# Strassen's algorithm in layer 0's queries and keys and its last two convolved blocks

## The chip, the cores and the metric

The kernel runs on one core of a Trainium2 chip. The metric is the device time of one execution in microseconds (us), as a median over runs; the profile shows one further execution of the same program.

## The reference

Two layers of a hybrid backbone over 256 context and 512 latent tokens of 1024 features, all in float32. Each layer normalises and modulates its input, multiplies it by one wide input projection, and feeds three groups of heads: a state space mixer (SSD) behind a three-tap convolution, differential attention, and latent attention (MLA). An output projection and an expert-choice mixture of 16 experts follow. What matters here is the input projection and what reads it first:

```python
ssd_l, diff_l, mla_l = jnp.split(h_lat @ w_in, cuts, axis=-1)
q, k, v = jnp.split(p, 3, axis=-1)                # differential attention, 256 columns each
k1 = jnp.concatenate([k1c, rope_2d(k1l, rows, cols)], axis=1)
xbc = jax.nn.silu(centred_dwconv(xbc, conv_w, conv_b))   # SSD: 512 columns of x, 128 of B, 128 of C
```

## The kernel before

`hT` holds the modulated rows of all 768 tokens, features on the partitions: 8 k-tiles of 128 features. Products that give features on the partitions take 128 columns of the projection as the stationary operand and tokens as the moving one (`feature_major`, L2468: two spans of 512 and 256 tokens, eight matmuls each); the values are made token by token (`token_major`, L2480).

Each engine has its own program, written out by hand in the order of the work, and they meet at semaphores. A PSUM slot is one of four tiles of 1024 floats; the jobs that use them are numbered by `job_plan` (L179) and job j has slot j modulo 4. `J.empty(j)` waits until the slot's last user has freed it, `J.filled(j)` and `J.freed(j)` for the job's own two steps. In layer 0 the queries and keys are jobs 11 to 14 ("qk"), their rotations 15 to 18 ("rot"), the values 19 and 20 ("v"). The convolved blocks are jobs x+0, 1, 3, 4, 5, 7 and the modulation rows (2, 1) and (2, 2) jobs x+2 and x+6.

Weights come through a ring of four buffers of 2 MB. SP issues the loads in the order of L822, and before it refills a buffer it waits in `block_used` (L788) for the last product with what lies there:

```python
for b in [*range(10), 11, 10, 12, 13, 15, 14, *range(16, PRE_BLOCKS)]:
```

Load 4 holds the weights of the queries and keys, 5 those of the values, 10 those of the first four convolved blocks, 15 those of the last two. Loads 12, 13, 14 and 16 hold modulation weights for `block_rows(l, 2, 0)` to `(l, 2, 3)` (L2497). Load b goes to buffer b modulo 4, so 14 goes where 10 was.

Layer 0 up to the first scores (TensorE L2638 to L2709): four blocks by `feature_major`, each followed by the rotation of the block before it (`quarter_turned`, L2640, one product with a constant matrix); values of four tiles, the last rotation, values of two tiles; then the first scores. ScalarE takes the queries and keys out of PSUM (L1167 to L1173): latents into `QK`, context heads into `QH` and `KH`. VectorE (L1682 to L1697) multiplies each block by cosines, its rotation by sines, and adds.

The convolved blocks of both layers come later (TensorE L2850 to L2894, VectorE L1862 to L1998, ScalarE L1301 to L1329). The first four are already made by Strassen's algorithm in Winograd's form: with tokens halved into 2 x 384, features into 2 x 512 and channels into pairs of blocks, seven products of half size take the place of eight. VectorE makes four sums of rows (`TH`, 1536 columns) and four of weights (`SW`, 1024), and joins the products out of PSUM by short sums of 384 columns. ScalarE copies the first product of a pair out (`E1`). These steps are counted by `half_products`, `half_sums` and `half_out`. Then, block by block in the order 2, 0, 3, 1, 4, 5, ScalarE scales with the middle tap, VectorE adds the other two taps (L1987) and ScalarE applies Silu. Blocks 4 and 5 are plain `feature_major` products, with `block_rows(l, 2, 2)` between them. Behind them on TensorE: sums over time, `block_rows(l, 2, 3)`, turned sums, the first gate with the columns of the modulation (`block_column`, which waits for VectorE's `rows_added(l, 2, 3)`), and the turning of all convolved blocks (L2931).

Of the kernel before, what the change touches and what calls it, by code (L numbers as in the profile page):

```python
# [24 lines left out]
P = 128  # L25
# [454 lines left out]
def build(nc, T, out):  # L480
    JOB = JOBS
    with ExitStack() as ctx:
# [117 lines left out]

        HT = TOK // 2
# [8 lines left out]
        CONV_ORDER = (2, 0, 3, 1, 4, 5)  # L610
# [431 lines left out]
        def _(act):  # L1042
# [109 lines left out]
            for l in range(DEPTH):  # L1152
# [14 lines left out]
                for m in range(4):  # L1167
                    j, scale = jb("qk") + m, DQ ** -0.5 if m < 2 else 1.0
                    act.wait_ge(*J.filled(j))
                    ins = act.activation(QK[:, m, CTX:TOK], J.tile(j)[:, CTX:TOK], ACT.Copy, scale=scale)  # L1170
                    if l == 0:
                        ins = context_heads_out(QH if m < 2 else KH, m % 2, J.tile(j)[:, 0:CTX], scale)
                    ins.then_inc(*J.free(j))  # L1173
# [127 lines left out]
                products0, sums0 = 10 * l, 22 * l  # L1301
# [11 lines left out]
                for i, m in enumerate(CONV_ORDER):  # L1313
                    j = conv_job(l, m)
                    if m in (2, 3):
                        act.wait_ge(S["half_sums"], sums0 + (15, 20)[m - 2])
                    elif m < 2:
                        act.wait_ge(*J.freed(conv_job(l, 2 * m + 1)))
                    else:
                        act.wait_ge(*J.filled(j))  # L1320
                    on = slice(conv_start(l, m), TOK)
                    src = CM[m] if m < 4 else J.tile(j)
                    act.activation(XB[:, m, on], src[:, on], ACT.Identity, bias=pc[:, R_CB + m:R_CB + m + 1],
                                   scale=pc[:, R_CW + CONV_T + m:R_CW + CONV_T + m + 1]).then_inc(S["conv_mid"], 1)
                    if m < 4:
                        act.wait_ge(S["half_sums"], sums0 + (16, 19, 21, 22)[i])
                    else:
                        act.wait_ge(*J.freed(j))
# [256 lines left out]
        def _(dve):  # L1585
# [56 lines left out]
            for l in range(DEPTH):  # L1642
# [33 lines left out]
                dve.tensor_reduce(lam[:, 128:130], view(lam[:, 0:64], a=2), AX_X, ALU.add).then_inc(S["lam_dots"], 1)  # L1676
                dve.wait_ge(*v.next(S["lam_exps"]))
# [4 lines left out]
                for m in range(4):  # L1682
                    dve.wait_ge(*J.freed(jb("qk") + m))
# [182 lines left out]
                sums0, out0, products0 = 22 * l, 2 * l, 10 * l  # L1866
# [1630 lines left out]
```

## Time and profile before

| | |
|---|---|
| three runs | 2092.53, 2095.02, 2096.34 us; median 2095.02 |
| profiled execution | 2094.3 us, span 2092.2 us, mean granted clock 0.988 |
| TensorE | matmuls in flight 1942.3 us (93%) |
| VectorE, ScalarE, GpSimd | 721.6 us (34%), 519.1 (25%), 186.9 (9%) |
| DMA | 530.64 MB, mean 254 GB/s |

Times in rows are us from the start of the span. A float32 matmul stands in the trace as two instructions. The length of a row of matmuls goes to the modelled end of its last one, which overlaps the next row; so the distance of two starts tells what work costs. "idle before" with an engine and a line is the time that the engine stood still, and what ended it. The clock is the granted clock of TensorE: 1.00 is 2.4 GHz, 0.5 is 1.2 GHz. A value between is a stretch with both.

### The profile page before, as it was taken

The page shows a single profiled execution, that of the slowest core. Times are in us where ns is not written, and L with a number is a line of the kernel's source. Part 1 is how long each engine was busy: PE and PEld are TensorE (multiplying, and loading weights), DVE is VectorE, ACT ScalarE, POOL GpSimd, SP SyncE. Part 2 cuts the span into 40 slices and gives each one's busy share as a digit, 9 for nine tenths or more (in the row PEclk, how much of TensorE's full clock was granted, in tenths as well). Part 3 has the DMA queues.
Part 4 walks back from the last instruction along what each step waited for, and adds up shares of the span by engine and source line. Part 5 has one row for each costly group of instructions (what it writes and reads, how often), then busy time and mean ns, then how long its engine had stood idle before and what let it go on. Part 6 is the DMA issues. An engine that isn't in the chain of part 4 may idle for free. (4 is left out here: it accounts for less than half of the span.)

```text
span 2092.2 us, 25952 instructions
## 1 busy us (share of the span) xinstructions
PE 1942.3 (93%) x10858; PEld 934.4 (45%) x10858; DVE 721.6 (34%) x1335; ACT 519.1 (25%) x1020; POOL 186.9 (9%) x216
## 2 busy tenths in 40 slices
PE   5998999989989999999999999999898998888886
PEld 2656565544433333333334866655445333232222
DVE  2258565372431110111113476563624111111113
ACT  4146552452300000000003255524321100000012
POOL 1300000120011111212012000001100000000000
PEclk9999999999999999999999999999999999999999
DMA  9520304222289999999999223024419999999996
GB/s 351 147 81 1 141 1 152 90 105 96 82 343 401 393 399 395 394 401 393 402 395 301 111 82 141 1 90 153 165 61 357 395 408 408 408 409 409 409 409 261
DMA packets 164805, 530.64 MB, mean 254 GB/s; under 512 B 11016, under 2 KB 19538, under 8 KB 164690
## 3 DMA queue, kind: packets, MB, share of 16 engines
q1 hardware_dynamic: 149344, 489.49, 60.0%
q0 software_dynamic: 15120, 39.43, 6.1%
q8 instruction: 87, 1.43, 0.3%
q14 instruction: 28, 0.23, 0.0%
q10 hardware_dynamic: 226, 0.07, 0.0%
HBM read 507.98 MB, written 20.97 MB: 253 GB/s over the span
## 5 line engine op out<-in xcount | busy, mean ns | idle before, releaser
L3267 PE MATMUL ps<-ring,arena 128*64 128x512 f32 x1040 | 233.2, 597 | 13.6 <-DMA ring<-in_w_up 8.8
L3267 PE MATMUL ps<-arena 128*64 128x512 f32 x720 | 165.0, 604 | 3.6 <-DMA arena<-in_w_gate 3.2
L3267 PEld LDWEIGHTS ps<-ring,arena 128*64 128x64 f32 x1040 | 72.1, 137 | 161.6 <-issue 141.3
L3093 PE MATMUL ps<-ring,arena 128*128 128x512 f32 x320 | 141.6, 597 | 1.0 <-ACT arena L1442 0.6
L2366 DVE TENSOR_TENSOR arena<-arena,ps 128x512 f32<-128x512 f32 x32 | 22.0, 688 | 280.1 <-ACT arena L1487 280.1
L3316 PE MATMUL ps<-ring,arena 128*64 128x512 f32 x496 | 112.4, 596 | 5.8 <-DMA ring<-in_w_down 5.8
L2476 PE MATMUL ps<-arena,ring 128*128 128x256 f32 (+1 forms) x384 | 110.4, 447 | 2.5 <-DMA ring<-in_w_in 2.5
L1487 ACT ACTIVATE arena<-ps 128x512 f32<-128x512 f32 x32 | 19.1, 597 | 373.4 <-PE ps L3267 373.4
L3316 PE MATMUL ps<-arena 128*64 128x512 f32 x432 | 97.9, 595 | 5.2 <-DMA arena<-in_w_down 4.5
L1066 ACT ACTIVATE arena<-ps 128x768 f32<-128x768 f32 (+6 forms) x111 | 79.9, 724 | 88.0 <-PE ps L2494 45.3
L3267 PEld LDWEIGHTS ps<-arena 128*64 128x64 f32 x720 | 50.4, 139 | 107.0 <-issue 100.3
L2476 PEld LDWEIGHTS ps<-arena,ring 128*128 128x128 f32 x384 | 73.2, 191 | 41.1 <-issue 31.5
L3093 PEld LDWEIGHTS ps<-ring,arena 128*128 128x128 f32 x320 | 59.7, 191 | 70.3 <-issue 69.5
L3216 PE MATMUL ps<-ring,arena 128*32 128x512 f32 x624 | 86.0, 594 | 0.4 <-DVE arena L2160 0.4
L2494 PE MATMUL ps<-const,arena 128*128 128x128 f32 x524 | 77.0, 283 | 7.9 <-DVE arena L1832 5.5
L1196 ACT ACTIVATE arena<-ps,nmax 128x768 f32<-128x768 f32 (+1 forms) x80 | 64.5, 811 | 60.6 <-DVE nmax L1715 56.1
L1715 DVE TENSOR_REDUCE nmax<-ps 128x1 f32<-128x768 f32 (+1 forms) x80 | 64.3, 846 | 39.8 <-PE ps L2682 38.9
L2494 PEld LDWEIGHTS ps<-const,arena 128*128 128x128 f32 x524 | 58.4, 143 | 42.5 <-issue 23.9
L2312 DVE TENSOR_TENSOR arena<-arena,ps 64x512 f32<-64x512 f32 x16 | 11.1, 692 | 188.7 <-ACT arena L1483 188.7
L2156 DVE TENSOR_TENSOR arena<-ps,coef 128x512 f32<-128x512 f32 (+1 forms) x48 | 28.8, 600 | 128.0 <-PE ps L3192 127.4
L3316 PEld LDWEIGHTS ps<-ring,arena 128*64 128x64 f32 x496 | 34.2, 137 | 77.3 <-issue 72.0
L914 POOL DMA_INDIRECT arena<-normed_rows,small x32 | 33.3, 1039 | 394.2 <-PE ps L3192 356.9
(417 smaller groups left out, 2821.8 us busy)
## 6 DMA issues: line engine op xcount, KB each, us to landing
ring<-in_w_up SPq DMA_DIRECT2D x33, 2048.0 KB, 14.7
ring<-in_w_gate SPq DMA_DIRECT2D x32, 2048.0 KB, 21.1
ring<-in_w_down SPq DMA_DIRECT2D x30, 2048.0 KB, 23.0
ring<-in_ada_w SPq DMA_DIRECT2D x24, 2048.0 KB, 9.9
arena<-in_w_down SPq DMA_DIRECT2D x19, 2048.0 KB, 23.2
arena<-in_w_gate SPq DMA_DIRECT2D x18, 2048.0 KB, 22.5
arena<-in_w_up SPq DMA_DIRECT2D x12, 2048.0 KB, 13.6
ring<-in_w_in SPq DMA_DIRECT2D x6, 2048.0 KB, 14.0
```

Source lines behind the costliest of these rows:

```text
L914: pool.indirect_dma_start(got_l[e % 2], None, halves_in, at_rows(e, 0)).then_inc(got_lat[e % 2], 16)
L1066: act.activation(dst, src, func, scale=scale).then_inc(*J.free(j))
L1196: act.activation(by_halves(PD[u % 2][m], t, nk // 2), by_halves(J.tile(j), t, 512), ACT.Exp, bias=nmax[:, c:c + 1], accum_out=esum[:, c:c ...
L1715: dve.tensor_reduce(nmax[:, c:c + 1], by_halves(J.tile(j), t, 512), AX_X if t < CT else AX_XY, ALU.max, negate=True).then_inc(S["negmax"], 1)
L2156: TT(x4, src.rearrange("p (c h n) -> p c h n", h=parts, n=n), cF[:, :, s].rearrange("p (h c) -> p c h", h=parts).unsqueeze(3) .to_broadcas ...
L2366: TT(hid_l, hid_l, px[0][:, 512:1024], ALU.mult).then_inc(S["hid_lat"], 1)
L2476: ins = mm(o[0:n, c0:c1], w[:, k, col:col + n], hT[:, k, c0:c1], start=k == 0, stop=k == KD - 1)
L2494: ins = pe.transpose(o[:, k * P:(k + 1) * P], src(k), ident)
L3093: ins = mm(o[:, hf * 512:(hf + 1) * 512], mix, wo[hf][:, k, :], start=k == 0, stop=k == KD - 1)
L3216: ins = mm(px[1][32 * i:32 * i + 32, 0:512], xc[e % 2][:, at:at + CAP_C], w[c][:, hf * 512:hf * 512 + 512], start=b + c == 0, stop=b * c == 3)
L3267: ins = mm(px[0][hf * 64:hf * 64 + 64, col:col + 512], xl[e % 2][:, at:at + CAP_L], w[c][:, hf * 512:hf * 512 + 512], start=b + c == 0, st ...
L3316: ins = mm(px[1][hf * 64:hf * 64 + 64, 512:1024], hT_l[0][:, at:at + CAP_L], w[c][:, hf * 512:hf * 512 + 512], start=b + c == 0, stop=b * ...
```

## The change

Layer 0's queries and keys are made by the same algorithm as the first convolved blocks, 14 products of four k-tiles and 384 tokens in place of four whole blocks; the pairs are blocks (0, 2) and (1, 3). VectorE makes eight sums from rows and weights and fourteen out of PSUM; ScalarE copies each pair's first product, later scales the latents of the query blocks in place, and copies the context heads from `QK`. Rotation 2 is put between the twelfth and the thirteenth product, rotation 0 behind the last product, 3 and 1 between the tiles of the values. The first scores wait for two roped blocks where they waited for three.

Layer 0's last two convolved blocks are made by seven such products. `block_rows(0, 2, 2)` stands behind the first of them. VectorE makes four sums of weights (512 columns each) within its turn for block 3; ScalarE copies the first product before its turn for block 1; the order of the blocks becomes 2, 0, 3, 1, 5, 4. In both layers `rows_added(l, 2, 1)` moves from behind block 1's taps to before `early_half(0)`; in layer 0 `rows_added(0, 2, 2)` moves before block 5's sums. SP's program is unchanged.

The diff, cut to its core, with eight columns of indentation taken off:

```diff
+def half_counts(l, conv):
+    return (25, 51, 9) if l else (10, 18, 6) if conv else (0, 0, 0)
+def qk_ready(m):
+    return S["half_out"], (4, 6, 3, 5)[m]
+QKH = (TOK - query_tiles(0)[0] * P) // 2
...
-CONV_ORDER = (2, 0, 3, 1, 4, 5)
+CM += [CM[0], CM[2]]
+CONV_ORDER = ((2, 0, 3, 1, 5, 4), (2, 0, 3, 1, 4, 5))
...
+            products0, sums0, _ = half_counts(l, 0)
+            for p in range(2):
+                act.wait_ge(S["half_products"], products0 + p + 1)
+                act.activation(EQ[p], J.tile(jb("qk") + 2 * p)[:, 0:QKH], ACT.Copy).then_inc(S["half_out"], 1)
+            for m in (2, 0, 3, 1):
+                scale = DQ ** -0.5 if m < 2 else 1.0
+                if m < 2:
+                    act.wait_ge(*J.freed(jb("qk") + 2 * m + 1))
+                    act.activation(QK[:, m, CTX:TOK], QK[:, m, CTX:TOK], ACT.Copy, scale=scale)
+                else:
+                    act.wait_ge(S["half_sums"], sums0 + (15 if m == 2 else 18))
+                context_heads_out(QH if m < 2 else KH, m % 2, QK[:, m, 0:CTX], scale).then_inc(S["half_out"], 1)
...
+            if l == 0 and m == 1:
+                act.wait_ge(S["half_products"], products0 + 11)
+                act.activation(E1[0], J.tile(conv_job(l, 4))[:, 0:HT], ACT.Copy).then_inc(S["half_out"], 1)
...
+        if l == 0:
+            qk_sum(TQ[0], qk_rows(0, 1), qk_rows(0, 0), ALU.subtract)
+            qk_sums_done(1)
+            qk_sum(TQ[1], qk_rows(4, 1), TQ[0], ALU.subtract)
+            dve.wait_ge(ring_full[n4 % RING], ring_turns(n4) * 16)
+            qk_sum(SQ[0], qk_weights(1, 0), qk_weights(1, 4))
+            qk_sums_done(3)
+            qk_sum(SQ[1], SQ[0], qk_weights(0, 0), ALU.subtract)
+            qk_sum(SQ[2], qk_weights(0, 0), qk_weights(1, 0), ALU.subtract)
+            qk_sum(TQ[2], qk_rows(4, 1), qk_rows(0, 1), ALU.subtract)
+            qk_sums_done(4)
+            qk_sum(SQ[3], qk_weights(0, 4), SQ[1], ALU.subtract)
+            qk_sum(TQ[3], qk_rows(4, 0), TQ[1], ALU.subtract)
+            for p in range(2):
+                dve.wait_ge(S["half_out"], out0 + p + 1)
+                dve.wait_ge(S["half_products"], products0 + 3 + p)
+                qk_sum(qk_out(p, 0), EQ[p], qk_tile(p, 0, 0))
+            for p in range(2):
+                dve.wait_ge(S["half_products"], products0 + 5 + p)
+                qk_sum(EQ[p], EQ[p], qk_tile(p, 0, 1))
+            for p in range(2):
+                qk_sums_done(11 + p)
+                dve.wait_ge(*J.filled(jb("qk") + 2 * p))
+                TT(UQ[p], EQ[p], qk_tile(p, 0, 1), ALU.add).then_inc(*J.free(jb("qk") + 2 * p))
...
+        def qk_late(p):
+            dve.wait_ge(*J.freed(jb("qk") + 2 * p))
+            dve.wait_ge(S["half_products"], products0 + 7 + 2 * p)
+            qk_sum(qk_out(2 + p, 1), UQ[p], qk_tile(p, 1, 0))
+            qk_sum(EQ[p], EQ[p], qk_tile(p, 1, 0))
+        def qk_early(p):
+            dve.wait_ge(S["half_products"], products0 + 8 + 2 * p)
+            qk_sum(qk_out(2 + p, 0), UQ[p], qk_tile(p, 1, 1))
+        def qk_last(p):
+            qk_sums_done((14, 17)[p])
+            dve.wait_ge(*J.filled(jb("qk") + 2 * p + 1))
+            TT(qk_out(p, 1), EQ[p], qk_tile(p, 1, 0), ALU.add).then_inc(*J.free(jb("qk") + 2 * p + 1))
+        if l == 0:
+            qk_late(0)
+            qk_early(0)
+            qk_last(0)
+            qk_late(1)
+        for i, m in enumerate(range(4) if l else (2, 0, 3, 1)):
+            if l == 0 and i == 1:
+                qk_early(1)
+                qk_last(1)
+            dve.wait_ge(*(J.freed(jb("qk") + m) if l else qk_ready(m)))
...
+        rows_added(l, 2, 1)
         early_half(0)
         last_half(0)
-        for m in CONV_ORDER:
+        def bc_weight_sums():
+            n15 = block_base(l) + 15
+            dve.wait_ge(ring_full[n15 % RING], ring_turns(n15) * 16)
+            wb15, s_ = ringv(n15), [last_pair_of_channels(x) for x in range(4)]
+            dve.wait_ge(*J.filled(conv_job(l, 2)))
+            half_sum(s_[0], wb15[:, 0:4, P:2 * P], wb15[:, 4:8, P:2 * P], ALU.add)
+            sums_done(21)
+            half_sum(s_[1], s_[0], wb15[:, 0:4, 0:P], ALU.subtract)
+            sums_done(22)
+            half_sum(s_[2], wb15[:, 0:4, 0:P], wb15[:, 0:4, P:2 * P], ALU.subtract)
+            half_sum(s_[3], wb15[:, 4:8, 0:P], s_[1], ALU.subtract)
+        def bc_halves():
+            j0, j1 = conv_job(l, 4), conv_job(l, 5)
+            dve.wait_ge(S["half_out"], out0 + 3)
+            rows_added(l, 2, 2)
+            dve.wait_ge(S["half_products"], products0 + 12)
+            half_sum(CM[4][:, 0:HT], E1[0], J.tile(j0)[:, 0:HT], ALU.add)
+            dve.wait_ge(S["half_products"], products0 + 13)
+            half_sum(E1[0], E1[0], J.tile(j0)[:, 512:512 + HT], ALU.add)
+            sums_done(28)
+            dve.wait_ge(*J.filled(j0))
+            TT(U3[0], E1[0], J.tile(j0)[:, 512:512 + HT], ALU.add).then_inc(*J.free(j0))
+            dve.wait_ge(*J.freed(j0))
+            half_sum(CM[5][:, HT:TOK], U3[0], J.tile(j1)[:, 0:HT], ALU.add)
+            half_sum(E1[0], E1[0], J.tile(j1)[:, 0:HT], ALU.add)
+            dve.wait_ge(S["half_products"], products0 + 15)
+            half_sum(CM[5][:, 0:HT], U3[0], J.tile(j1)[:, 512:512 + HT], ALU.add)
+            sums_done(30)
+            dve.wait_ge(*J.filled(j1))
+            TT(CM[4][:, HT:TOK], E1[0], J.tile(j1)[:, 0:HT], ALU.add).then_inc(*J.free(j1))
...
+        for m in CONV_ORDER[l]:
             j = conv_job(l, m)
             if m == 0:
                 late_half(1)
             if m == 3:
                 early_half(1)
+                if l == 0:
+                    bc_weight_sums()
                 last_half(1)
+            if m == 5 and l == 0:
+                bc_halves()
...
-            if m in (1, 4):
-                rows_added(l, 2, m // 2 + (m == 1))
+            if l and m == 4:
+                rows_added(l, 2, 2)
...
+            def qk_product(p, i, hf, a, b, k0=None):
+                o = J.tile(jb("qk") + 2 * p + i)[:, 512 * hf:512 * hf + n]
+                for k in range(4):
+                    if k0 is not None:
+                        first_h(k0 + k)
+                    ins = mm(o, a[:, k, :], b[:, k, :], start=k == 0, stop=k == 3)
+                return ins
+            def of_qk_pair(x, p):
+                return SQ[x][:, :, P * p:P * p + P]
+            for p in range(2):
+                pe.wait_ge(*J.empty(jb("qk") + 2 * p))
+                qk_product(p, 0, 0, qk_weight(p, 0, 0), qk_rows(0, 0), 0 if p == 0 else None).then_inc(S["half_products"], 1)
+            for p in range(2):
+                pe.wait_ge(S["half_out"], out0 + p + 1)
+                qk_product(p, 0, 0, qk_weight(p, 0, 4), qk_rows(4, 0), 4 if p == 0 else None).then_inc(S["half_products"], 1)
+            pe.wait_ge(S["half_sums"], sums0 + 4)
+            for p in range(2):
+                qk_product(p, 0, 1, of_qk_pair(1, p), TQ[1]).then_inc(S["half_products"], 1)
+            for p in range(2):
+                pe.wait_ge(S["half_sums"], sums0 + 11 + p)
+                qk_product(p, 0, 1, of_qk_pair(2, p), TQ[2]).then_inc(*J.fill(jb("qk") + 2 * p))
+            for p in range(2):
+                pe.wait_ge(*J.empty(jb("qk") + 2 * p + 1))
+                qk_product(p, 1, 0, of_qk_pair(0, p), TQ[0]).then_inc(S["half_products"], 1)
+                if p:
+                    quarter_turned(l, 2)
+                qk_product(p, 1, 1, qk_weight(p, 1, 4), TQ[3]).then_inc(S["half_products"], 1)
+                pe.wait_ge(S["half_sums"], sums0 + (14, 17)[p])
+                qk_product(p, 1, 0, of_qk_pair(3, p), qk_rows(4, 1)).then_inc(*J.fill(jb("qk") + 2 * p + 1))
+            quarter_turned(l, 0)
...
-            token_major(jb("v"), w[:, :, 0:256], range(0, 4), 256, 256)
-            quarter_turned(3)
+            token_major(jb("v"), w[:, :, 0:256], range(0, 4), 256, 256, between={1: 3, 2: 1})
             token_major(jb("v") + 1, w[:, :, 0:256], range(4, 6), 256, 256)
             pe.wait_ge(*J.freed(jb("v") + 1))
-        pe.wait_ge(*w_.next(S["qk_roped"], 3))
+        pe.wait_ge(*w_.next(S["qk_roped"], 3 if l else 2))
...
+            pe.wait_ge(*J.empty(conv_job(l, 4)))
+            bc_product(0, 0, w[:, 0:4, 0:P], rows_half(0, 0)).then_inc(S["half_products"], 1)
+            block_rows(l, 2, 2)
+            pe.wait_ge(S["half_out"], out0 + 3)
+            bc_product(0, 0, w[:, 4:8, 0:P], rows_half(4, 0)).then_inc(S["half_products"], 1)
+            pe.wait_ge(S["half_sums"], sums0 + 24)
+            bc_product(0, 1, last_pair_of_channels(1), TH[1]).then_inc(S["half_products"], 1)
+            pe.wait_ge(*J.empty(conv_job(l, 5)))
+            bc_product(1, 0, last_pair_of_channels(0), TH[0]).then_inc(S["half_products"], 1)
+            pe.wait_ge(S["half_sums"], sums0 + 28)
+            bc_product(0, 1, last_pair_of_channels(2), TH[2]).then_inc(*J.fill(conv_job(l, 4)))
+            bc_product(1, 1, w[:, 4:8, P:2 * P], TH[3]).then_inc(S["half_products"], 1)
+            pe.wait_ge(S["half_sums"], sums0 + 30)
+            bc_product(1, 0, last_pair_of_channels(3), rows_half(4, 1)).then_inc(*J.fill(conv_job(l, 5)))
```

The counts of the semaphores in layer 1 and in the convolution are shifted by what the new steps add; nothing else of layer 1's products changes.

## Rows read from the trace of the kernel before

**Rows 1.** The page: span, and busy time of TensorE, VectorE, ScalarE and GpSimd.

```profile
span 2092.2 us, 25952 instructions
...
PE 1942.3 (93%) x10858; PEld 934.4 (45%) x10858; DVE 721.6 (34%) x1335; ACT 519.1 (25%) x1020; POOL 186.9 (9%) x216
```

**Rows 2.** Windows of the experts: length, busy PE, PEld, DVE, ACT, POOL, clock, DMA.

```profile
800.00:900.00 100.00, 100.00 (x718) 36.06 (x716) 13.29 (x24) 7.41 (x12) 16.00 (x12) 1.00 1.03 397
...
1800.00:2092.00 292.00, 241.75 (x987) 79.92 (x985) 58.51 (x89) 32.84 (x57) 4.85 (x6) 0.97 0.96 383
```

**Rows 3.** Timeline of TensorE, layer 0's queries, keys, values: start, length, what, count [idle].

```profile
41.54 22.60 PE L2476 MATMUL ps<-arena,ring 128*128 128x512 f32 x64 [2.45 <-DMA ring<-in_w_in]
...
63.98 1.02 PE L2645 MATMUL ps<-arena,const 128*128 128x512 f32 x2
64.84 10.48 PE L2476 MATMUL ps<-arena,ring 128*128 128x512 f32 x32
75.16 1.02 PE L2645 MATMUL ps<-arena,const 128*128 128x512 f32 x2
...
109.63 0.70 PE L2682 MATMUL ps<-arena,resid 32*128 32x256 f32 x4 [0.69 <-ACT arena L1066]
```

**Rows 4.** Timeline of TensorE, layer 0, from the convolution's products to the turned blocks.

```profile
341.33 2.74 PE L2865 MATMUL ps<-arena 128*128 128x384 f32 x8
343.91 10.48 PE L2476 MATMUL ps<-arena,ring 128*128 128x512 f32 x32
354.32 1.92 PE L2508 MATMUL ps<-ring,silu_c 128*32 128x512 f32 x16
...
366.60 0.32 PE L2900 MATMUL ps<-small,const 128*128 128x48 f32 x2
...
374.15 0.28 PE L2532 MATMUL ps<-const,mod_rows 128*128 128x8 f32 x2
...
381.44 0.29 PE L2936 MATMUL ps<-const,arena 128*128 128x2 f32 x2
```

**Rows 5.** Timeline of VectorE beside the convolution of layer 0.

```profile
306.09 3.55 DVE L1881 TENSOR_TENSOR arena<-arena 128x1536 f32<-128x1536 f32 x2
...
317.56 0.55 DVE L1881 TENSOR_TENSOR arena<-arena,ps 128x384 f32<-128x384 f32 x1
...
343.31 0.55 DVE L1881 TENSOR_TENSOR arena<-arena,ps 128x384 f32<-128x384 f32 x1
344.18 0.56 DVE L1933 TENSOR_TENSOR resid<-arena,ps 128x384 f32<-128x384 f32 x1 [0.33 <-PE ps L2865]
345.22 2.33 DVE L1987 SCALAR_TENSOR_TENSOR resid<-arena,par,resid 128x255 f32<-128x255 f32 x4 [0.48 <-ACT resid L1323]
349.37 2.33 DVE L1987 SCALAR_TENSOR_TENSOR resid<-resid,par 128x255 f32<-128x255 f32 x4 [1.83 <-ACT resid L1323]
351.61 0.68 DVE L1615 TENSOR_TENSOR mod_rows<-ps,mod_rows 128x512 f32<-128x512 f32 x1
```

**Rows 6.** SP's timeline, then the transfers issued from 343.9 to 344.3 with landing.

```profile
344.10 0.99 SPq L835 DMA_DIRECT2D ring<-in_ada_w  x2
...
ring<-in_ada_w SPq DMA_DIRECT2D x1, 2048.0 KB, 7.8
```

**Rows 7.** Timeline of VectorE beside layer 0's queries and keys.

```profile
44.44 0.22 DVE L1676 TENSOR_REDUCE lam<-lam 128x2 f32<-128x64 f32 x1
...
65.77 2.79 DVE L1695 TENSOR_TENSOR resid<-arena 64x512 f32<-64x512 f32 x4
...
88.12 2.78 DVE L1695 TENSOR_TENSOR arena<-arena 64x512 f32<-64x512 f32 x4
```

**Rows 8.** Windows: beside the queries and keys, and around TensorE's idle at 1501.

```profile
44.40:68.00 23.60, 23.60 (x70) 13.36 (x69) 4.12 (x10) 4.18 (x11) 23.25 (x40) 0.96 0.81 203
...
1500.90:1504.20 3.30, 0.07 (x1) 0.00 (x0) 0.77 (x3) 3.08 (x13) 0.00 (x0) 0.91 0.59 237
1504.20:1510.80 6.60, 5.59 (x35) 4.51 (x36) 2.23 (x4) 1.74 (x5) 2.73 (x5) 0.53 0.79 302
```

More of the change, by code:

```diff
@@ L609, in build, with last_pair_of_channels, plain @@
         assert h0 + 4 * HT + TOK <= h1 - 704
-        CONV_ORDER = (2, 0, 3, 1, 4, 5)
+        CM += [CM[0], CM[2]]
+        CONV_ORDER = ((2, 0, 3, 1, 5, 4), (2, 0, 3, 1, 4, 5))
+        def last_pair_of_channels(x):
+            return SW[1 + x // 2][:, :, P * (x % 2):P * (x % 2) + P]
+        def plain(l, m):
+            return l > 0 and m >= 4
         XC = 640 + SG
@@ L2478, in feature_major, with quarter_turned, token_major @@
                             ins.then_inc(*J.fill(j))
-            def token_major(j, w, tiles, n, stride, at=0):
+            def quarter_turned(l, m):
+                j = JOB[l, "rot"] + m
+                pe.wait_ge(*(J.freed(JOB[l, "qk"] + m) if l else qk_ready(m)))
+                pe.wait_ge(*J.empty(j))
+                mm(J.tile(j)[:, 0:SEQ], kc(K_ROT), QK[:, m, CTX:TOK], start=True, stop=True).then_inc(*J.fill(j))
+            def token_major(j, w, tiles, n, stride, at=0, between={}):
                 pe.wait_ge(*J.empty(j))
@@ L2484, in token_major @@
                 for i, t in enumerate(tiles):
+                    if i in between:
+                        quarter_turned(0, between[i])
                     for k in range(KD):
@@ L2638, in _, with qk_weight, qk_rows @@
                 w = arrived(wb + 4)
-                def quarter_turned(m):
-                    j = jb("rot") + m
-                    pe.wait_ge(*J.freed(jb("qk") + m))
-                    pe.wait_ge(*J.empty(j))
-                    mm(J.tile(j)[:, 0:SEQ], kc(K_ROT), QK[:, m, CTX:TOK], start=True, stop=True).then_inc(*J.fill(j))
-                for m in range(4):
-                    feature_major(jb("qk") + m, w, m * P, P, t0,
-                                  ready=(latents_ready if l else first_h) if m == 0 else None)
-                    if m:
-                        quarter_turned(m - 1)
+                if l:
+                    for m in range(4):
+                        feature_major(jb("qk") + m, w, m * P, P, t0,
+                                      ready=latents_ready if m == 0 else None)
+                        if m:
+                            quarter_turned(l, m - 1)
+                else:
+                    _, sums0, out0 = half_counts(l, 0)
+                    n, c0 = QKH, t0 * P
+                    def qk_weight(p, half, k0):
+                        return w[:, k0:k0 + 4, 256 * half + P * p:256 * half + P * p + P]
+                    def qk_rows(k0, half):
+                        return hT[:, k0:k0 + 4, c0 + half * n:c0 + half * n + n]
+                    def qk_product(p, i, hf, a, b, k0=None):
[28 more added lines that the diff above has]
+                    quarter_turned(l, 0)
@@ L2675, in map_scores @@
                     if u == 2 * nq:
-                        pe.wait_ge(*w_.next(S["qk_roped"]))
+                        pe.wait_ge(*w_.next(S["qk_roped"], 1 if l else 2))
                     for m in range(2):
```

78 lines of the change are left out of this document (52 added, 26 removed).

## The prediction, made before the change was run

> **What bounds the kernel now.** I read the page first: the span is 2092.2 us and TensorE has matmuls in flight for 93% of it [rows 1]. The table by windows then says what an early saving is worth: in the expert stage of layer 0 TensorE never idles, and the end of layer 1 runs at the rate of the weight transfers (a DMA share of 0.96 with TensorE at 242 of 292 us) [rows 2]. Those transfers refill buffers that TensorE lets go, so an earlier or later TensorE in layer 0's mixer moves everything behind it one for one. I take that as the price of every microsecond below; its other bound is that the transfers hide it, which would only draw the result towards zero. Only TensorE's timeline in the two changed stretches counts, then: queries and keys with the values behind them [rows 3], and the last two convolved blocks with what follows [rows 4].
>
> **First part: queries and keys.** A block of 768 columns and eight k-tiles took 75.16 - 64.84 = 10.32 us [rows 3]. The kernel already does its first four convolved blocks by Strassen, and one product there (four k-tiles, 384 columns) took 343.91 - 341.33 = 2.58 us [rows 4]. Four blocks, 41.28 us, become 14 products, 36.12 us: **-5.16 us**. The four rotations stay, at 0.9 each.
>
> Do the sums come in time? I carried the old starting point: the first two blocks took 22.4 us where two take 20.6, so 1.8 us go at the start at the lower clock, in both versions. Product n then ends at 43.34 + 2.58n: product 4 at 53.7, product 6 at 58.8. VectorE is free after the reduction at 44.44 [rows 7]. The same eight sums took 317.56 - 306.09 = 11.47 us in the convolution [rows 5], the fourth being done halfway. Here the fourth is done at 50.6 (needed at 53.7), the eighth at 56.1; the three short ones behind it (0.5 us each, row 343.31) put the one that product 7 needs at 57.6, against 58.8. So there is no wait, with 1.2 us to spare. Block 2 (keys) is whole behind product 10 (69.1), ScalarE copies its context heads by 71.5, and its rotation comes at 74.3: no wait. The second pair follows the same pattern 7.7 us later, with the same covers.
>
> A new wait stands at the values. The job of the values has the PSUM slot of rotation 0 (19 and 15 modulo 4), and VectorE frees it only after the last product's sum. Product 14 ends at 80.3 (with rotation 2's 0.9); the sum reads it 0.27 later (344.18 - 343.91), takes 0.5, then cosine and sine product, 0.68 each as the row at 351.61: 82.5. TensorE has done rotation 0 at 81.2: **+1.3 us**. Rotations 3 and 1, now between value tiles, find their halves copied and their slots free (81 to 84 against 86 and 90). The rope additions (2.8 us a block) end near 95, the values near 105, and the first scores wait for ScalarE's copy of the values as before, 109.63 being 3.85 us too late now. Net **-3.85 us**.
>
> **Second part: the last two convolved blocks.** I keep the old times here; all of it comes 3.85 us earlier. Two blocks, 20.64 us, become seven products, 18.06 us: -2.6 us. But the order on TensorE changes as well. block_rows(0, 2, 2), which multiplies modulation weights from the ring, stood behind a whole convolved block (354.32 [rows 4]); now it stands behind one product, at 343.91 + 2.58 = 346.49. Its weights are load 14, in ring slot 2, where load 10 (the weights of the first four blocks) was; SP may refill it only when the last product with load 10 is done. The queue shows that: it issued at 344.10, and the 2 MB landed 7.8 us later, at 351.9 [rows 6]. Before, this was hidden by 2.4 us; now TensorE waits **5.4 us**, and everything is queued behind it in order. The change doesn't touch SP's order.
>
> That wait covers the other one. The copy E1[0], which product 2 needs, stands in ScalarE's queue behind block 3's Silu, which waits for VectorE's taps, and those now stand behind four new weight sums. From row 343.31: 0.5, four sums of 128x512 at some 0.7 (row 351.61, the nearest), 0.5, taps 2.24 (351.61 - 349.37), Silu and copy 1.3: 350.6, before 351.9. It costs nothing here; without the transfer it would be 350.6 - 346.5 - 1.9 = 2.3 us.
>
> So TensorE: 351.9 + 1.9 (row 354.32) + 6 x 2.58 = 369.2, against 366.60: **+2.6 us**. In these products each sum is ready at least 0.6 us ahead.
>
> Behind it, the end E of the convolution starts a chain for the two last blocks: last sum at E + 0.27, 0.5; taps of block 5, 2.24; Silu and scaling to the next taps 1.9 (349.37 - 345.22 - 2.24 [rows 5]); taps of block 4, 2.24; row addition 0.68; handed over at E + 7.9. TensorE asks for the finished rows at 374.15 - 366.60 = 7.55: **+0.35 us**. The turned blocks are asked for at E + 14.8 (381.44) and ready at E + 9: free. POOL and the next SP loads start some us later and have more than that to spare. The earlier row addition frees the PSUM slot that block_rows(l, 2, 2) needs, 0.7 us of VectorE in a gap; in layer 1, where nothing else changes, nobody waited there, so nothing.
>
> **The clock.** TensorE idle for 3.3 us at 1500.9 came back to 6.6 us at 0.53, the 1.2 GHz level, and then worked at 2.4 again [rows 8]. A 5.4 us idle stretch will do the like. Bounds are 0 and half of 6.6, 3.3 us; the work here is dense at once, unlike at 1504, so I take **+1.7 us**. The Trainium skill, "TensorE: Matmul & The Clock Gate", What's actually happening, calls the throttled state the default that activity releases; by that rule the fall would come here too, and the trace agrees.
>
> **Sum:** -3.85 + 2.6 + 0.35 + 1.7 = +0.8 us on 2094.3, the profiled execution's time (2.1 over its span, which I keep); that run stood 0.7 below the median of 2095.0, so the forecast is **2095.8 us**: no difference that can be told. A measurement here tells some 0.2%, 4.2 us, from nothing; the three runs lie 3.8 apart.
>
> **Rivals.**
> 1. *The transfer doesn't hold TensorE* (lands by 348.8). Then the copy's wait of 2.3 decides, the clock stays: -3.85 - 2.6 + 2.3 + 0.35 = -3.8, 2091.2. Against it: it would have to land 4.7 us after its issue where it took 7.8, or be released earlier, and the only thing that releases it is the last product. 0.10, half of it over the bound.
> 2. *Everything is hidden*: -5.2 - 2.6, 2087.2. Needs a free slot at the values and no wait in the convolution; the rows speak against both. 0.06.
> 3. *Slower: VectorE's sums come too late.* Place: before product 7, margin 1.2 us. POOL issues small loads from 44.7 to 68, just beside the eight sums; were the sums half as long again (5.7 us), TensorE would wait 4.5 and the time be 2100.3; doubled, 2106. It decides from sums 10% longer, and is slower than the bound from 40%. Against: four additions beside POOL's issues took 2.79 us (65.77), without them 2.78 (88.12) [rows 7]. 0.10. The Trainium skill, "SBUF — State Buffer", Who interferes with whom, says that a VectorE instruction with two SBUF inputs and a GpSimd instruction that reads SBUF block each other whole; by that rule this is the case to fear, but the trace shows no such stretch for queue issues.
>
> **Numbers.** The forecast case has 0.74. Its own spread (clock 0 to 3.3, values' wait 0 to 2.5, runs +-1.5) is 2092.5 to 2099; with rival 1 and the nearest of rival 3 the range is **2091.0 to 2099.5**. Faster by over 0.2%: 0.12; within: 0.76; slower: 0.12.
>
> **What would show it.** Right: TensorE idle some 5 us before line block_rows in the convolution, put down to the ring's transfer, then a stretch of clock near 0.5; the first scores 3.9 us earlier; 1 to 2 us idle before the values, behind VectorE. Wrong: sums above 1.9 us beside POOL; a wait before product 7; transfer 14 issued before the last product with load 10; a gap before the turned blocks.

## The result, and the profile after

The change makes the kernel slower: 2104.5 us in the median of ten runs (2099.1 to 2111.2), where ten runs of the kernel before, taken beside them, have 2095.7. The ratio is 1.0041, with a 95% interval of 1.0031 to 1.0051. The forecast was 2095.8 us with no difference to tell, and its range ended at 2099.5. The profiled execution took 2104.57 us, 10.3 above that of before.

The page of the kernel after, its span and the busy times:

```profile
span 2102.1 us, 25949 instructions
...
PE 1943.6 (92%) x10834; PEld 932.6 (44%) x10834; DVE 746.6 (36%) x1368; ACT 520.1 (25%) x1021; POOL 187.5 (9%) x216
```

Against [rows 1] TensorE has 24 fewer matmul records and 1.3 us *more* busy time: a first sign that some of its work ran at the lower clock. VectorE has 25 us more to do.

TensorE's timeline of the kernel after in the front stretch (start, length, what, count, [idle before]); these answer to [rows 3]:

```profile
41.51 12.28 PE L2829 MATMUL ps<-arena,ring 128*128 128x384 f32 x32 [2.39 <-DMA ring<-in_w_in]
53.63 5.32 PE L2829 MATMUL ps<-arena 128*128 128x384 f32 x16
58.79 5.32 PE L2829 MATMUL ps<-resid,arena 128*128 128x384 f32 x16
...
80.29 1.02 PE L2641 MATMUL ps<-arena,const 128*128 128x512 f32 x2
82.47 3.69 PE L2651 MATMUL ps<-ring,arena 128*128 128x256 f32 x16 [1.15 <-DVE arena L1805]
...
105.83 0.48 PE L2886 MATMUL ps<-arena,resid 32*128 32x256 f32 x2 [0.69 <-ACT arena L1089]
```

And VectorE's, the first row of the eight sums, and the three short sums behind them:

```profile
44.61 3.54 DVE L1733 TENSOR_TENSOR arena<-arena 128x1536 f32<-128x1536 f32 x2
...
56.08 1.48 DVE L1733 TENSOR_TENSOR arena<-arena,ps 128x384 f32<-128x384 f32 x3
```

The whole first part stands as it was worked out. TensorE never waits among the products; the eight sums take 56.08 - 44.61 = 11.47 us, to the hundredth what they take in the convolution [rows 5], although GpSimd issues its loads beside them (it is busy for 11.32 of the 11.5 us from 44.6); the wait before the values is 1.15 us and ends with VectorE's sine product (L1805); the first scores start at 105.83, 3.80 us earlier than in [rows 3].

TensorE's timeline after, from the convolution's last products to the turned blocks, against [rows 4]:

```profile
340.12 2.74 PE L3105 MATMUL ps<-arena,ring 128*128 128x384 f32 x8
348.48 3.64 PE L2673 MATMUL ps<-ring,silu_c 128*32 128x512 f32 x16 [5.62 <-DMA ring<-in_ada_w]
352.05 3.33 PE L3105 MATMUL ps<-arena,ring 128*128 128x384 f32 x8
...
368.12 0.32 PE L3127 MATMUL ps<-small,const 128*128 128x48 f32 x2
...
374.31 0.47 PE L3143 MATMUL ps<-const,arena 128*32 128x128 f32 x8
377.76 2.04 PE L3150 MATMUL ps<-ring,arena 128*128 128x512 f32 x2 [2.98 <-DVE small L2164]
...
388.96 0.29 PE L3163 MATMUL ps<-const,arena 128*128 128x2 f32 x2
```

The first gap is the one foretold: 5.62 us before `block_rows(0, 2, 2)` (L2673), put down to the ring's transfer. SP's queue and the transfer itself answer to [rows 6]: issued at 340.31, when the last product with the old weights is done, landed 8.0 us later.

```profile
340.31 0.99 SPq L858 DMA_DIRECT2D ring<-in_ada_w  x2
...
ring<-in_ada_w SPq DMA_DIRECT2D x1, 2048.0 KB, 8.0
```

The second gap, 2.98 us before the first gate (L3150), the forecast doesn't have. Its releaser is VectorE's L2164, the copy of the sums over time out of PSUM. VectorE's timeline after, from the end of the convolution:

```profile
368.39 0.56 DVE L2124 TENSOR_TENSOR arena<-arena,ps 128x384 f32<-128x384 f32 x1 [2.09 <-PE ps L3105]
368.86 2.32 DVE L2143 SCALAR_TENSOR_TENSOR resid<-arena,par,resid 128x255 f32<-128x255 f32 x4
373.01 2.33 DVE L2143 SCALAR_TENSOR_TENSOR resid<-arena,par,resid 128x255 f32<-128x255 f32 x4 [1.83 <-ACT resid L1364]
375.26 0.68 DVE L1659 TENSOR_TENSOR mod_rows<-ps,mod_rows 128x512 f32<-128x512 f32 x1
376.25 0.96 DVE L2158 TENSOR_TENSOR arena<-resid 128x768 f32<-128x768 f32 x1 [0.31 <-ACT resid L1370]
377.13 0.32 DVE L2163 COPY small<-ps 128x48 f32<-128x48 f32 x2
377.36 0.25 DVE L2164 COPY small<-ps 128x96 f32<-128x96 f32 x1
```

What these small copies hold up isn't their data. The sums over time are job `cum`; the first gate is four jobs on and so has the same PSUM slot, and TensorE can't write it before the copies have emptied it. TensorE made the sums at 368.12, but VectorE reads them after both last blocks' taps, the row addition and the product of B and C. In the kernel before only one block's taps stood there, and the copies were done at 372.41, 0.8 us ahead of the first gate:

```profile
371.93 0.32 DVE L2007 COPY small<-ps 128x48 f32<-128x48 f32 x2
372.16 0.25 DVE L2008 COPY small<-ps 128x96 f32<-128x96 f32 x1
...
373.19 1.13 PE L2923 MATMUL ps<-ring,arena 128*128 128x512 f32 x2
```

The granted clock beside both gaps, and at a later place (windows of the kernel after; the clock is the number before the last two):

```profile
346.60:353.40 6.80, 4.92 (x19) 1.61 (x20) 2.98 (x5) 1.83 (x3) 0.00 (x0) 0.52 1.05 387
377.40:384.20 6.80, 6.44 (x13) 3.40 (x14) 0.73 (x4) 2.90 (x8) 1.04 (x1) 0.53 0.53 195
442.20:445.60 3.40, 3.40 (x14) 1.49 (x11) 1.93 (x3) 1.66 (x2) 0.91 (x1) 0.55 0.00 0
```

All three are near 0.5, the 1.2 GHz level; the kernel before has none between 132 and 1142 us. TensorE's way from the gap's end to the end E of the convolution took 368.12 - 348.48 = 19.64 us where 1.85 + 6 x 2.58 = 17.33 would do: 2.3 us for the first. From the gate to the turned blocks it took 11.20 us where before has 381.44 - 373.19 = 8.25: 2.95 for the second.

The balance of the two profiles, after minus before, at places where both do the same thing (before's times: first scores and E in [rows 3, 4]; the gate at 373.19; the turned blocks in [rows 4]; the first modulation columns of layer 1 at 1131.2; the spans in [rows 1]):

| place | before | after | difference |
|---|---|---|---|
| first scores | 109.63 | 105.83 | -3.80 |
| end E of the convolution | 366.60 | 368.12 | +1.52 |
| first gate | 373.19 | 377.76 | +4.57 |
| turned blocks | 381.44 | 388.96 | +7.52 |
| start of layer 1 | 1131.2 | 1140.8 | +9.6 |
| end of the span | 2092.16 | 2102.13 | +9.97 |

From the turned blocks on the two programs are the same in layer 0. Of the last 2.4 us, 1.8 come by 599 us; about the half of the 3.4 us at the lower clock at 442, 1.7 us, is that much. TensorE had stood idle just before that stretch, but it does so in the kernel before as well (1.88 us, up to 433.52), and there the clock stayed full:

```profile
441.03 1.36 PE L3198 MATMUL ps<-resid 32*128 32x512 f32 x8 [1.89 <-issue]
```

### The profile page after: what moved, and what is told of

Same layout as the page of the kernel before. It is cut to its first block and busy times, and to the rows that moved or that the text cites. A ratio compares the mean times of both kernels' runs of the same rounds, so it can differ in the third digit from the quotient of the medians.

```text
span 2102.1 us, 25949 instructions
## 1 busy us (share of the span) xinstructions
PE 1943.6 (92%) x10834; PEld 932.6 (44%) x10834; DVE 746.6 (36%) x1368; ACT 520.1 (25%) x1021; POOL 187.5 (9%) x216
## 5 line engine op out<-in xcount | busy, mean ns | idle before, releaser
L3320 PE MATMUL ps<-ring,arena 128*128 128x512 f32 x320 | 141.7, 597 | 1.0 <-ACT arena L1483 0.6
L2522 DVE TENSOR_TENSOR arena<-arena,ps 128x512 f32<-128x512 f32 x32 | 22.0, 687 | 281.1 <-ACT arena L1528 281.1
L2491 DVE TENSOR_TENSOR arena<-arena,ps 128x512 f32<-128x512 f32 x48 | 32.9, 687 | 95.2 <-PE ps L3475 95.1
L3212 PE MATMUL ps<-ring,arena 128*128 128x512 f32 x128 | 63.8, 634 | 0.8 <-ACT arena L1436 0.5
## 6 DMA issues: line engine op xcount, KB each, us to landing
arena<-in_w_up SPq DMA_DIRECT2D x12, 2048.0 KB, 13.9
ring<-in_w_in SPq DMA_DIRECT2D x6, 2048.0 KB, 13.6
```

Source lines behind the costliest of these rows:

```text
L2491: TT(dst, dst, src, ALU.add).then_inc(S["sums_out"], 1)
L3212: ins = mm(ps[2][:, 512:1024], hT[:, k, tok], wz[:, k, :], start=k == 0, stop=k == KD - 1)
L3320: ins = mm(o[:, hf * 512:(hf + 1) * 512], mix, wo[hf][:, k, :], start=k == 0, stop=k == KD - 1)
```

## The experiments

The theory, W in the expectations, is this: the first part pays 3.8 to 4 us as worked out; the second costs about twelve, by four steps (transfer, clock, the PSUM slot of the sums over time, clock), and the two waits come from nothing but the order of the work. The rival puts the loss elsewhere: into the first part's after-effects, or into VectorE's extra work. All kernels were timed in five rounds beside the kernel before (medians of 2095.1 us beside experiments 1 to 4 and 2095.8 beside 5 to 8, of 29 runs each; 2095.7 beside the change). Differences between two versions in us are of their medians unless a ratio is named. The ratios to the kernel before give some of them otherwise by some 3 us; where the argument rests on one, both stand there. The interval of a difference of two ratios is an estimate, the root of the sum of the squares of their half widths.

**1. The first part alone.** Layer 0's last two blocks are plain again; the queries and keys stay.

```diff
-        CONV_ORDER = ((2, 0, 3, 1, 5, 4), (2, 0, 3, 1, 4, 5))
+        CONV_ORDER = ((2, 0, 3, 1, 4, 5), (2, 0, 3, 1, 4, 5))
...
-            return l > 0 and m >= 4
+            return m >= 4
...
-    if m == 5 and l == 0:
-        bc_halves()
```

> The first part alone: Strassen in layer 0's queries and keys, the last two convolved blocks as before (the earlier row addition of part (2, 1) stays). Theory W (two waits behind the new convolved blocks make the whole loss: for the transfer of load 14, and for the PSUM slot of the first gate, each with a fall of the clock): the first scores start 3.8 us earlier than before and all of that is kept to the end, so the time is 3 to 4.5 us below the kernel before (some 2092, ratio 0.998), and TensorE's idle before block_rows(0, 2, 2) is gone. Rival S (the sums on VectorE and the moved rotations cost something further on that is not seen at the first scores, as the 2.4 us lost between 389 us and the end suggest): not below the kernel before.

Measured: 2093.05 us, ratio 0.9993 (0.998 to 1.0006). The profile keeps the saving up to the turned blocks (377.39 against 381.44, -4.05) and has no wait at the gate (369.14, 6.58 behind its end of the convolution, E). Then it loses it, for the most part at places where the profile of before has full clock; windows of this kernel:

```profile
431.30:434.70 3.40, 3.40 (x9) 1.32 (x8) 2.78 (x3) 1.51 (x2) 1.94 (x2) 0.58 0.00 0
468.80:475.60 6.80, 6.80 (x19) 4.32 (x19) 1.92 (x2) 0.20 (x1) 0.90 (x2) 0.54 1.02 413
591.70:595.10 3.40, 3.40 (x12) 2.55 (x9) 0.93 (x4) 1.87 (x2) 1.93 (x2) 0.58 1.03 411
```

By 590 us it is 0.3 behind before, and at the end 1.2 ahead. So the first part is not the loss, and its 4 us are in the profile; in the median some 2 us are left, not clear of noise.

**2. The second part alone.** The queries and keys are plain again.

```diff
-    for p in range(2):
-        pe.wait_ge(*J.empty(jb("qk") + 2 * p))
-        qk_product(p, 0, 0, qk_weight(p, 0, 0), qk_rows(0, 0), 0 if p == 0 else None).then_inc(S["half_products"], 1)
...
+for m in range(4):
+    feature_major(jb("qk") + m, w, m * P, P, t0,
+                  ready=(latents_ready if l else first_h) if m == 0 else None)
+    if m:
+        quarter_turned(l, m - 1)
```

> The second part alone: the last two convolved blocks as seven products, queries and keys plain as before. Theory W: slower than the kernel before by 12 to 14 us (8.8 measured for the whole change plus 3.85), some 2108: idle of 5.4 to 5.8 us before block_rows(0, 2, 2) put down to the ring's transfer, 3 us idle before the first gate put down to VectorE, and two stretches at the lower clock. Rival S: slower by less than 9 us.

Measured: 2103.56 us, ratio 1.0054 (1.0037 to 1.0072). By the medians that is +8.4 us, by the ratio +11.3 with an interval of some 8 to 15. So the second part alone brings the whole loss; but six runs don't tell the 12 to 14 that were expected from the less than 9 of the rival. TensorE's timeline has both waits:

```profile
351.94 3.64 PE L2643 MATMUL ps<-ring,silu_c 128*32 128x512 f32 x16 [5.55 <-DMA ring<-in_ada_w]
...
380.97 1.10 PE L3074 MATMUL ps<-ring,arena 128*128 128x512 f32 x2 [2.97 <-DVE small L2134]
```

The clock falls only once here, as the windows show:

```profile
349.70:356.50 6.80, 4.56 (x18) 1.37 (x19) 2.99 (x5) 2.26 (x4) 0.00 (x0) 0.53 1.05 387
381.00:387.80 6.80, 6.80 (x22) 3.60 (x23) 0.37 (x2) 2.98 (x8) 1.04 (x1) 1.00 0.47 171
```

So the wait of 2.97 us stands in every profile of this order behind E (experiments 3 and 7 have it too), and the fall of the clock only in some. With the full clock the gate leads to the turned blocks (389.19) in 8.22 us, as in the kernel before.

**3. The transfer's wait taken away by order.** The products that don't need load 14 go ahead of `block_rows(0, 2, 2)`: the work is the same, in another order; the row addition moves with it.

```diff
-    block_rows(l, 2, 2)
-    pe.wait_ge(S["half_out"], out0 + 3)
-    bc_product(0, 0, w[:, 4:8, 0:P], rows_half(4, 0)).then_inc(S["half_products"], 1)
     pe.wait_ge(S["half_sums"], sums0 + 24)
     bc_product(0, 1, last_pair_of_channels(1), TH[1]).then_inc(S["half_products"], 1)
     pe.wait_ge(*J.empty(conv_job(l, 5)))
     bc_product(1, 0, last_pair_of_channels(0), TH[0]).then_inc(S["half_products"], 1)
+    pe.wait_ge(S["half_out"], out0 + 3)
+    bc_product(0, 0, w[:, 4:8, 0:P], rows_half(4, 0)).then_inc(S["half_products"], 1)
+    block_rows(l, 2, 2)
```

> The whole change, with TensorE's order in the last two convolved blocks changed: products 1, 3, 4, 2 (those that need no copy first), then block_rows(0, 2, 2), then 5, 6, 7; VectorE's rows_added(0, 2, 2) behind its second sum. Theory W: TensorE is 4.4 us beyond the release of load 10's buffer when it asks for load 14's weights instead of 2.6, that is at 354.2 in the old times against a landing at 351.9, so that idle (5.6 us) and the first fall of the clock (2.3 us) go; the wait before the first gate (3 us) stays with its fall of the clock. 7 to 9 us less than the changed kernel, 2096 to 2098. If the transfer isn't the cause: no difference over 2 us.

Measured: 2095.65 us, ratio 1.0008 (0.9998 to 1.0018), 8.8 us under the change; by the ratios 6.9, with an interval of some 4 to 10. TensorE's timeline:

```profile
351.70 1.92 PE L2672 MATMUL ps<-ring,silu_c 128*32 128x512 f32 x16
...
361.40 0.32 PE L3126 MATMUL ps<-small,const 128*128 128x48 f32 x2
...
371.03 1.94 PE L3149 MATMUL ps<-ring,arena 128*128 128x512 f32 x2 [2.98 <-DVE small L2163]
```

The modulation rows start with no idle before them, E is at 361.40, 5.2 us ahead of before, and the second wait has stayed at 2.98. A stretch of 3.4 us at the lower clock (0.51 from 371.1 to 374.5) goes with it.

**4. The slot of the sums over time freed earlier.** In layer 0 VectorE copies them ahead of the last block's taps, in the time in which it waits for ScalarE; the transfer's wait stays.

```diff
+    if m == 4 and l == 0:
+        cums_out()
...
-j = jb("cum")
-dve.wait_ge(*J.filled(j))
...
+if l:
+    cums_out()
```

> The whole change, with VectorE's three copies of the sums over time (which free the PSUM slot that the first gate needs) moved from behind the last block's Silu to before the last block's taps. Theory W: the idle of 3.0 us before the first gate goes, and with it the second stretch at the lower clock (6.8 us long, 3.2 us lost); the transfer's wait stays. 4 to 6.5 us less than the changed kernel, 2098 to 2100. A rival: the first gate then waits for the finished modulation rows instead (row addition at the end of the same chain, 0.35 us by the prediction), so that no more than 3 us are won.

Measured: 2098.83 us, ratio 1.0027 (1.0013 to 1.0042). The median is 5.6 us under the change, but the ratios differ by 2.9 us only, with an interval of some -1 to 7: by its time alone the gain isn't clear of noise. Four of the twelve runs took 2104.9 to 2105.6 us, the others 2095.4 to 2099.2. TensorE's timeline at the gate:

```profile
381.73 1.13 PE L3157 MATMUL ps<-ring,arena 128*128 128x512 f32 x2
383.01 0.39 PE L2704 MATMUL ps<-const,mod_rows 128*128 128x8 f32 x2 [0.16 <-DVE mod_rows L1659]
```

The gate follows E by 6.59 us with no wait, as in the kernel before. What the prediction priced at 0.35, the row addition handed over too late, shows now, since nothing hides it any more: an idle row of 0.16 us, and the turned blocks (390.40) 8.67 us behind the gate where before has 8.25, so 0.42 in all. Against the change's profile that is 3.05 - 0.42 of waiting and 2.95 of clock less, 5.6; that the medians differ by just as much is chance. What the time gains is told better by experiments 3 and 5, which differ by this edit alone. The profiled execution (span 2102.8 us) is one of the four long runs, because of something else, 13.6 us at the lower clock while TensorE was busy throughout; a window of this kernel:

```profile
227.80:241.40 13.60, 13.60 (x20) 4.80 (x19) 5.97 (x8) 4.26 (x6) 3.33 (x4) 0.51 0.20 64
```

**5. Both mends together**, edits 3 and 4 on the change.

> The whole change with both mends of e3 and e4: the order 1, 3, 4, 2 ahead of block_rows(0, 2, 2), and the copies of the sums over time before the last block's taps. Theory W: neither wait is left, so the turned blocks start at 381.4 - 3.85 (queries and keys) - 2.6 (one product of eight saved in two blocks) + 0.4 (modulation rows) = 375.4, 6 us before the kernel before; no fall of the clock between 300 and 390. The end is blurred by falls of the clock further on, which e1 showed to take back up to 4 us in single runs: ratio to the kernel before 0.997 (0.996 to 0.9985), 2089 to 2092. If something else of the new convolution costs time: above 2094.

Measured: 2089.4 us, ratio 0.9977 (0.9964 to 0.999): faster than before by 6.4 us and than the change by 15 (by the ratios 4.8 and 13, the latter within some 10 to 17). Under experiment 3, from which it differs by the early copies alone, it lies by 6.3 us, by the ratios by 6.5 with an interval of some 3 to 10. TensorE's timeline:

```profile
351.66 1.92 PE L2679 MATMUL ps<-ring,silu_c 128*32 128x512 f32 x16
...
361.36 0.32 PE L3133 MATMUL ps<-small,const 128*128 128x48 f32 x2
...
367.95 1.12 PE L3156 MATMUL ps<-ring,arena 128*128 128x512 f32 x2
```

And VectorE's, with the copies between the taps of the two blocks:

```profile
362.10 2.32 DVE L2155 SCALAR_TENSOR_TENSOR resid<-arena,par,resid 128x255 f32<-128x255 f32 x4
364.34 0.32 DVE L2131 COPY small<-ps 128x48 f32<-128x48 f32 x2
```

Neither wait is left, the clock is full at both places, and the turned blocks start at 376.63, 12.3 us earlier than in the change: 5.62 + 2.3 and 2.98 + 2.95 of waits and clock are 13.9 in the change's profile; 1.0 is lost again before the first scores (106.80) and 0.4 to the late row addition. VectorE's work is as large as in the change (745.8 us busy), so its amount was not the loss; the order was.

**6. The values' wait taken away as well.** On top of 5, rotation 0 goes before the last product, VectorE frees its slot before it turns to the last sums, and rotations 3 and 1 come one tile of values later.

```diff
+        if p:
+            quarter_turned(l, 0)
         pe.wait_ge(S["half_sums"], sums0 + (14, 17)[p])
         qk_product(p, 1, 0, of_qk_pair(3, p), qk_rows(4, 1)).then_inc(*J.fill(jb("qk") + 2 * p + 1))
-    quarter_turned(l, 0)
```

> e5 with rotation 0 ahead of the fourteenth product, its sine product and additions on VectorE ahead of the second pair's last sums, and rotations 3 and 1 one tile of values later. If the wait at the values is for the PSUM slot of rotation 0, as the trace has it, the idle of 1.15 us before the first value tile goes and the first scores start at 104.7 instead of 105.8; the end 1 us below e5, within the noise of the clock. If the values wait for something else, the first scores start no earlier.

Measured: 2090.59 us, ratio 0.998 (0.9966 to 0.9994). TensorE's timeline:

```profile
81.20 7.07 PE L2657 MATMUL ps<-ring,arena 128*128 128x256 f32 x32
...
104.49 0.70 PE L2893 MATMUL ps<-arena,resid 32*128 32x256 f32 x4 [0.69 <-ACT arena L1089]
```

The wait is gone and the first scores come at 104.49, 1.3 us earlier than in the change. The time doesn't tell it from version 5: the runs of one kernel lie wider apart than that.

**7. TensorE kept busy in the transfer's gap.** The first of the seven products is made three times over, with the same operands; everything else is the change. If the lower clock came with the transfer, or with the place, it would stay; if TensorE's idle time brings it, it goes.

```diff
+    bc_product(0, 0, w[:, 0:4, 0:P], rows_half(0, 0))
+    bc_product(0, 0, w[:, 0:4, 0:P], rows_half(0, 0))
     bc_product(0, 0, w[:, 0:4, 0:P], rows_half(0, 0)).then_inc(S["half_products"], 1)
```

> The whole change, with the first of the seven products made three times over (the same product, the first two overwritten), so that TensorE works through 5.2 of the 5.6 us for which it waits for load 14. Nothing is left out. It tells the cost of the clock from that of the wait. If the fall of the clock at 346.6 is brought by the idle stretch: it is gone, block_rows(0, 2, 2) takes 1.9 instead of 3.6 us, the sums over time start at 365.8 instead of 368.1, and the time is some 2 us below the changed kernel, though TensorE does more. The wait before the first gate stays at 3 us. If the clock has another cause: no change of the end of the convolution.

Measured: 2100.72 us, ratio 1.0035 (1.0022 to 1.0048). The median is 3.8 us under the change, but of six runs, and the ratios differ by 1.3 us with an interval of some -2 to 5: the time doesn't tell whether it is faster. It isn't shown to be slower either, with 5.2 us more of work. What the experiment tells stands in the trace. TensorE's timeline and two windows of the clock:

```profile
339.64 7.90 PE L3105 MATMUL ps<-arena,ring 128*128 128x384 f32 x24
347.96 1.92 PE L2673 MATMUL ps<-ring,silu_c 128*32 128x512 f32 x16 [0.41 <-DMA ring<-in_ada_w]
...
365.40 0.32 PE L3129 MATMUL ps<-small,const 128*128 128x48 f32 x2
...
375.03 1.33 PE L3152 MATMUL ps<-ring,arena 128*128 128x512 f32 x2 [2.97 <-DVE small L2164]
```

```profile
346.60:353.40 6.80, 6.38 (x30) 2.89 (x30) 3.45 (x6) 2.25 (x3) 0.00 (x0) 1.00 1.05 387
...
376.40:379.80 3.40, 3.40 (x7) 1.81 (x8) 0.00 (x1) 1.69 (x3) 1.03 (x1) 0.59 0.53 196
```

The transfer is as it was and the clock stays full. E comes at 365.40, 2.7 us earlier: 2.2 of the clock (365.40 - 347.96 = 17.44 from the gap's end on, for 19.64), and 0.5 because all was that much earlier already at the first product (339.64 for 340.12), the transfer too.

**8. The second part alone, with both mends**: edits 3 and 4 on version 2.

> The second part alone (queries and keys plain) with both mends. Theory W: turned blocks at 381.4 - 2.6 + 0.4 = 379.2; ratio to the kernel before 0.999 (0.998 to 1.0); against e2, the same part without the mends, 8 to 10 us less.

Measured: 2094.47 us, ratio 0.9995 (0.9986 to 1.0003), 9.1 us under version 2 (by the ratios 12, within some 8 to 16); the gate (371.84) follows E (365.25) by 6.59 us, and the turned blocks come at 380.52, for 379.2 expected. The mends undo the loss without the first part's help. By the medians the second part alone then gives about 1 us, and the first alone about 2, neither clear of noise; together they gave 6.4, with an interval of 2 to 7.5 that the sum of the two lies in.

## Why the prediction was wrong

**Right, step by step.** The price of a product, 2.58 us; the sums beside GpSimd's issues, done at 56.08 against 56.1 worked out; no wait before product 7; the wait at the values, 1.15 for 1.3; the first scores at 105.83 for 105.78. In the convolution the transfer's wait, 5.62 for 5.4, with its cause; the copy E1[0] out by 346.67 and hidden (worked out: 350.6 less the 3.85 by which all is earlier, 346.75); the row addition handed over at 375.94, E + 7.82 (worked out: E + 7.9). The fear of rival 3 had a rule beside it: the Trainium skill, "SBUF — State Buffer", Who interferes with whom, has a VectorE instruction with two SBUF inputs contend with a GpSimd instruction that reads SBUF. Whether GpSimd's issues are such instructions no run here tells; the eight sums took 11.47 us with them and without.

**The step that failed** is the walk behind E. It followed the chain up to the row addition and then said "The turned blocks are asked for at E + 14.8 (381.44) and ready at E + 9: free." Between the two TensorE asks for something else: an empty slot for the first gate, at E + 6.6. The copies that empty it stand in VectorE's queue behind all that the chain names, and behind the product of B and C; they end at 377.61, E + 9.5. The prediction had found just such a wait at the values, through the slot of rotation 0, and didn't look for the next one: it asked when data would be ready and not when space would. In the kernel before, the same copies were only 0.8 us ahead of the gate, so a second block's taps in front of them had to show. Experiment 4 takes this wait away alone, as its trace shows; in the time the same edit, between experiments 3 and 5, is worth 6.3 us (by the ratios 6.5, interval 3 to 10). In the profile of the change it is 3.05 us of waiting, which hides the 0.35 foreseen, and 2.95 us of clock.

**The term that was too small** is the clock. 1.7 us for one fall, within bounds of 0 to 3.3; the fall took 2.3, and there was a second, of 2.95, behind the second wait: 5.25 in this profile. The rule was cited in the right sense: the Trainium skill, "TensorE: Matmul & The Clock Gate", What's actually happening, calls the throttled state the default that activity releases. Here the gap of some 5.6 us was followed by a low stretch in each of the three profiles that have it (the change, experiments 2 and 4), and in none of the seven without it (the kernel before and experiments 1, 3, 5, 6, 7 and 8). In experiment 7 only TensorE's idleness had been filled; it is one profile.

**The sum again**, to the turned blocks: the forecast has -3.85 + 2.6 + 1.7 + 0.35 = 0.8. Measured are 1.07 us more at E (0.6 of clock, 0.2 of the transfer, the rest in steps under 0.1), 2.7 for the slot beyond the 0.35, and 2.95 of clock: 7.5. Behind them another 2.4 were lost, 1.8 of them to the low stretch at 442. That this stretch is the change's own isn't shown: experiments 1, 5, 7 and 8 have one too, at 429 to 438, and the kernel before and experiments 2, 3, 4 and 6 have none there. The idle of 1.9 us in front of it stands in all ten profiles.

**One microsecond for one** was the price of an early saving. The experts hide nothing, as [rows 2] said: the +9.3 us at 599 are +9.6 at 1141 and +9.97 at the end. But a saving isn't safe in transit either; experiment 1 carried 4.05 us to 377 and had lost them by 590, for the most part to low clock. How much of that is chance, one profile of each kernel can't say; it stays open.

**The rivals and the range.** None of the three came true. Rivals 1 and 2 had less waiting than the forecast, and rival 3 had VectorE's sums late in the first part; none was a slot behind the convolution. The range was also narrower than its own terms: added up, 1.6 of clock, 1.2 at the values and 1.5 of the runs lead from 2095.8 to 2100.1, not 2099; that wouldn't have reached the result either. With the failed step in, the sum would have been 2094.3 + 0.8 + 2.7 + 2.95 = 2100.8, still 3.8 short of the profiled run: 1.07 of it at E, and the rest behind the turned blocks. The chance of 0.12 for slower came for the most part from rival 3, and the case that came had none of its own.

## What to carry to other kernels

When work is reordered on an engine that runs in order, list for every later instruction the *empty* buffer that it needs as well as its data, and find who frees it and what stands in that engine's queue now; numbered jobs on four slots make that a mechanical walk. Where products don't depend on a late load, put them ahead of the one that does: here that order was worth some 7 to 9 us, as much as the 7.8 us of products that the algorithm saves. A gap ahead of dense work on TensorE can be paid up to twice through the clock (5.62 + 2.3 and 2.98 + 2.95 in the change, 2.97 + 0 in experiment 2). Work that fills it can keep the clock, even useless work, as experiment 7's trace shows; that this made the kernel faster isn't shown.

## What was unexpected of the hardware

A short wait of 2.98 us in front of dense work brought 6.8 us at the lower clock in one profile, 3.4 us in two (experiments 3 and 7, where gate to turned blocks took 9.91 us in place of 8.22), and none in a fourth (experiment 2): the same order of work may meet either. Shorter idle has such stretches behind it as well, in some profiles: the 1.9 us before 433.5 in the kernel before (441.03 in the change) stand in all ten, and a low stretch of 3.4 us begins within 1.3 us of their end in five (the change, experiments 1, 5, 7 and 8). What decides between the two stays open. One low stretch appears without idle near it, the 13.6 us at 227.8 in experiment 4: TensorE was busy through all of it and for 22.6 of the 22.8 us before it. Single runs of the unchanged kernel lie between 2088 and 2099 us, wider than what most single edits here were worth, and the shortest has the highest mean clock (0.991 for 2088.14 us).
